# One core, a hybrid mLSTM / gMLP / memory-attention layer with experts: the second half of the memory keys in two units of 512 rows by 512 columns, and a different order of gate weights, gate rows and outputs in one DMA queue

## The reference

```
mk_p, mv_p = memory_kv(mem_prompt, mem_norm_g, w_mem_k, w_mem_v)   # rmsnorm(mem) @ w_k, @ w_v: (256 x 1024) @ (1024 x 1024) each
z = rmsnorm(x) @ w_in                     # 1024 x 10248: q,k,v,o, gate columns i,f, u, gv, memory queries, branch gates
ig = i_raw + i_b; lf = log_sigmoid(f_raw + f_b)      # 4 heads, cumulative sum and running maximum over time
...                                       # mLSTM scan, gMLP, attention of the memory queries over mk, mv
x = x + mixed @ w_out
x = x + hier_moe(rmsnorm(x), ...)         # 4 groups x 8 experts, top 2
```

## Time and profile before

| | before |
|---|---|
| median of 3 executions | 840.59 us (840.16 to 841.1) |
| profiled execution, its own time | 841.19 us |
| profiled execution, span from the first to the last instruction | 839.4 us |
| PE, DVE, ACT busy | 98%, 70%, 56% of the span |
| mean granted TensorE clock | 0.998 |

### The profile page before, as it was taken

The page is one execution under the profiler, slowest core; times in us unless marked ns, Lnnn a source line. Parts: engine busy times, 40 slices in busy tenths (PEclk is TensorE's granted clock), DMA queues, the critical chain, the costliest instruction groups (busy, mean ns, idle before and its releaser), DMA issues. The chain is left out here.

```text
span 839.4 us, 12162 instructions
## 1 busy us (share of the span) xinstructions
PE 823.4 (98%) x4744; PEld 732.3 (87%) x4744; DVE 586.7 (70%) x820; ACT 469.1 (56%) x622; POOL 62.8 (7%) x113
## 2 busy tenths in 40 slices
PE   7999999999999999999999999999999999999995
PEld 7979989988989998899999999878888888888884
DVE  5665487773445456695565456778989889889894
ACT  5645577754333324554333336656877768767773
POOL 1000100010000000000000000020004102210410
PEclk9999999999999999999999999999999999999999
DMA  8659855327534536345436467589999999999970
GB/s 269 208 142 291 221 142 132 118 81 220 165 126 126 176 115 199 126 151 163 152 110 216 151 201 256 209 264 409 389 357 351 358 397 381 352 373 366 382 279 18
DMA packets 111841, 191.83 MB, mean 229 GB/s; under 512 B 18692, under 2 KB 76960, under 8 KB 111648
## 3 DMA queue, kind: packets, MB, share of 16 engines
q1 hardware_dynamic: 109824, 185.91, 65.0%
q0 software_dynamic: 1152, 3.41, 1.1%
q10 hardware_dynamic: 800, 1.66, 0.6%
HBM read 181.70 MB, written 10.03 MB: 228 GB/s over the span
## 5 line engine op out<-in xcount | busy, mean ns | idle before, releaser
L1643 DVE TENSOR_TENSOR w_r<-arena,w_r 128x2048 fp32r<-128x2048 f32 x96 | 217.0, 2286 | 27.6 <-ACT w_r L1239 27.6
L1634 DVE TENSOR_TENSOR unit_r<-arena,unit_r 128x2048 fp32r<-128x2048 f32 x63 | 144.3, 2291 | 131.2 <-ACT unit_r L1228 131.1
L793 PE MATMUL pj<-xn_r,unit_r 128*128 128x320 f32 x1536 | 233.2, 311 | 0.8 <-issue 0.8
L793 PEld LDWEIGHTS pj<-xn_r,unit_r 128*128 128x128 f32 x1536 | 225.6, 188 | 4.7 <-issue 3.7
L1130 PE MATMUL pj<-w_r,xg 128*128 128x512 f32 x768 | 191.0, 398 | 0.5 <-DVE xg L1627 0.4
L1239 ACT ACTIVATE w_r<-arena 128x2048 fp32r<-128x2048 f32 x96 | 180.3, 1909 | 2.7 <-DMA arena<-in_w_exp_down 2.0
L1130 PEld LDWEIGHTS pj<-w_r,xg 128*128 128x128 f32 x768 | 141.8, 188 | 31.5 <-DVE xg L1627 0.8
L1228 ACT ACTIVATE unit_r<-arena 128x2048 fp32r<-128x2048 f32 x63 | 120.9, 1919 | 44.4 <-PE pj L793 23.6
L1159 PE MATMUL pj<-w_r,hidT 128*128 128x512 f32 x384 | 93.3, 392 | 0.6 <-ACT hidT L1490 0.6
L1159 PEld LDWEIGHTS pj<-w_r,hidT 128*128 128x128 f32 x384 | 71.8, 188 | 17.0 <-issue 0.8
L793 PE MATMUL pj<-br_r,unit_r 128*128 128x320 f32 x384 | 59.6, 311 | 0.0
(11 more groups left out here) (344 smaller groups left out, 793.3 us busy)
## 6 DMA issues: line engine op xcount, KB each, us to landing
arena<-in_w_in SPq DMA_DIRECT2D x40, 1024.0 KB, 5.5
arena<-in_w_exp_gate SPq DMA_DIRECT2D x64, 512.0 KB, 4.9
arena<-in_w_exp_up SPq DMA_DIRECT2D x64, 512.0 KB, 6.7
arena<-in_w_exp_down SPq DMA_DIRECT2D x64, 512.0 KB, 5.6
arena<-in_w_mem_v SPq DMA_DIRECT2D x4, 1024.0 KB, 5.3
arena<-in_w_br_mem SPq DMA_DIRECT2D x4, 1024.0 KB, 5.1
arena<-in_w_br_mlstm SPq DMA_DIRECT2D x4, 1024.0 KB, 5.1
arena<-in_w_br_gmlp SPq DMA_DIRECT2D x4, 1024.0 KB, 4.9
```

The costliest lines, as they stand in the source:

```text
L793: last = mm(bank_of(s)[0:out_rows, 0:out_cols], l, r, start=k == 0, stop=k == len(pairs) - 1)
L1634: v.tensor_tensor(unit_part(n, 1), raw_columns(n), unit_part(n, 0), ALU.subtract).then_inc(u_lo, 1)
L1643: v.tensor_tensor(w_r[u % NS][:, 1, :], raw_w[u % NS], w_r[u % NS][:, 0, :], ALU.subtract).then_inc(m_lo, 1)
```

## The change

The units 2 and 3 (columns 512 to 1023 of `w_mem_k`) become a wide pair `memk2`, as the memory values already are: unit 2 is rows 0 to 511, unit 3 rows 512 to 1023, each by 512 columns. The number of units and of MB stays. In SP's queue `load_gate_weights` moves from ahead of unit 3 to behind unit 4; the write of the gate rows stays behind unit 10 but the read that spreads them moves behind unit 11; the memory keys are stored behind unit 11, the two maxima behind unit 12, the memory values behind unit 14; the wait ahead of the prompt keys is for the two key stores alone.

```diff
@@ -97,11 +97,12 @@
                 step(kind, u, kh, i, ring="pj", eng=engs[i], unit=n, last=i == tiles - 1, held=kh == 0, of=(kind, u, 0, i) if kh else None)
                 after(u, kh, i)
 
-    for u in range(4):
+    for u in range(2):
         n = unit("w_mem_k", u * 256)
         for i in range(2):
             step("memk", u, i, ring="pj", eng="A", unit=n, last=i == 1)
             early.pop(0)()
+    wide("memk2", "w_mem_k", 0, 1, 2, "AA", lambda u, kh, i: early.pop(0)())
     for u in range(2):
         wide("memv", "w_mem_v", 0, u, 2, "AA", lambda u, kh, i: early.pop(0)())
     step("paramsync", ring=None, eng=None)
@@ -630,22 +632,27 @@
                 sp.dma_start(wrb[:, 0:G], I["b_router_group"][0, :].partition_broadcast(128)).then_inc(s_par3, 16)
                 sp.dma_start(wrb[:, G:G + E], I["b_router_expert"][0, :].partition_broadcast(128)).then_inc(s_par3, 16)
 
-            def spread_gate_rows():
+            def write_gate_rows():
 
                 sp.wait_ge(s_g4, 1)
                 sp.dma_start(spread_rows, rb[0:H, :]).then_inc(s_rbw, 16)
+
+            def spread_gate_rows():
+
                 sp.wait_ge(s_rbw, 16)
                 sp.dma_start(rbb[:, :, :].rearrange("p h t -> p (h t)"), spread_rows.rearrange("h t -> (h t)").partition_broadcast(128)).then_inc(s_rbb, 16)
 
-            def store_memory():
+            def store_maxima():
 
                 sp.wait_ge(s_g3, 1)
                 sp.dma_start(O["mlstm_m_prompt"][0, 0, :].rearrange("(h a) -> h a", a=1), rows[0:H, R_MM, TP - 1:TP]).then_inc(s_mout, 16)
                 sp.dma_start(O["mlstm_m_sample"][0, 0, :].rearrange("(h a) -> h a", a=1), rows[0:H, R_MM, T - 1:T]).then_inc(s_mout, 16)
+
+            def store_memory(name, src):
+
                 sp.wait_ge(*done("memv", 1, 1, 1))
-                for name, src in (("mem_k_prompt", memk), ("mem_v_prompt", memv)):
-                    for i in range(2):
-                        sp.dma_start(O[name][0, 0, i * 128:(i + 1) * 128].rearrange("p h d -> p (h d)"), src[:, i, :]).then_inc(s_memout, 16)
+                for i in range(2):
+                    sp.dma_start(O[name][0, 0, i * 128:(i + 1) * 128].rearrange("p h d -> p (h d)"), src[:, i, :]).then_inc(s_memout, 16)
 
             def store_conv():
 
@@ -700,7 +707,6 @@
                     for i, (t0, rows_) in enumerate(TILES):
                         src = I["x_prompt"][0, t0:t0 + rows_, :] if i < 2 else I["x_sample"][0, :, :]
                         sp.dma_start(x_tm[0:rows_, i, :], src).then_inc(s_x, 16)
-                    load_gate_weights()
                 if n == 0:
                     continue
                 if n >= 3:
@@ -709,19 +715,26 @@
                 r0 = part[0] * 512 if part else 0
                 src = I[name][0, r0:r0 + UW // w * 128, col:col + w].rearrange("(k p) n -> p k n", p=128)
                 sp.dma_start(raw_unit[unit_slot(n)].rearrange("p (k n) -> p k n", n=w), src).then_inc(unit_full[unit_slot(n)], 16)
-                if n == 6:
+                if n == 4:
+                    load_gate_weights()
+                elif n == 6:
                     sp.dma_start(ws[:, :, :], I["gmlp_w_s"][0].rearrange("g t s -> t g s")).then_inc(s_ws, 16)
                 elif n in (8, 9):
                     load_cached_keys(n - 8)
                     load_cache_v(n - 8)
                 elif n == 10:
+                    write_gate_rows()
+                elif n == 11:
                     spread_gate_rows()
-                elif n == 11:
-                    store_memory()
+                    store_memory("mem_k_prompt", memk)
+                elif n == 12:
+                    store_maxima()
                 elif n == 13:
-                    sp.wait_ge(s_memout, 64)
+                    sp.wait_ge(s_memout, 32)
                     load_prompt_keys(0)
                     load_prompt_keys(1)
+                elif n == 14:
+                    store_memory("mem_v_prompt", memv)
                 elif n in (16, 18):
                     sp.wait_ge(s_kmT, n - 14)
                     load_cached_keys(n // 2 - 6)
@@ -890,7 +903,7 @@
                             pe.wait_ge(u_lo, 1)
                         for m, (p, q) in enumerate(PARTS):
                             last = mm(b[:, 0:256], mn_r[:, p, k, a[1] * 128:a[1] * 128 + 128], w[:, q, k, :], start=k + m == 0, stop=k == KC - 1 and m == 2)
-                elif kind == "memv":
+                elif kind in ("memk2", "memv"):
                     u, kh, i = a
                     last = project_half(s, 128, kh, 3, lambda k, m: (mn_r[:, PARTS[m][0], 4 * kh + k, i * 128:i * 128 + 128], w[:, PARTS[m][1], k, :]))
                 elif kind in ("v", "gv"):
@@ -1314,9 +1327,9 @@
                     if a == (0, 0):
                         act.wait_ge(s_rsm, 1)
                     af(memk[:, a[1], a[0] * 256:a[0] * 256 + 256], b[:, 0:256], ACT.Copy, scale=rs[:, 3 + a[1]:4 + a[1]]).then_inc(free, 1)
-                elif kind == "memv" and mine:
+                elif kind in ("memk2", "memv") and mine:
                     u, _, i = a
-                    af(memv[:, i, u * 512:u * 512 + 512], b[:, 0:512], ACT.Copy, scale=rs[:, 3 + i:4 + i]).then_inc(free, 1)
+                    af((memk if kind == "memk2" else memv)[:, i, u * 512:u * 512 + 512], b[:, 0:512], ACT.Copy, scale=rs[:, 3 + i:4 + i]).then_inc(free, 1)
                 elif kind == "mq":
                     af(mqT[:, a[0], :], b[:, 0:T], ACT.Copy, scale=QSCALE).then_inc(free, 1)
                 elif kind == "sc":
```

## The result

| | before | changed |
|---|---|---|
| median | 840.85 us (840.05 to 842.34, 6 runs) | 845.19 us (844.07 to 845.69, 6 runs) |
| profiled execution, its own time | 841.19 us | 845.69 us |
| span | 839.4 us | 843.9 us |
| mean granted TensorE clock | 0.998 | 0.994 |

The ratio is 1.0049, with a 95% interval of 1.0036 to 1.0062: the change makes the kernel about 4.3 us slower. My 842.3 and my range up to 844.2 were too low.

A forecast was written before the change was run, and what follows sets the result against it. TensorE (PE), busy 98%, was taken to bound the kernel; -1.67 us in front and +3.43 us from a longer gap ahead of unit 10 gave +1.76 us, so 842.3 us, range 839.1 to 844.2.

The forecast's parts named there:

- What bounds the kernel: Whole kernel: TensorE is busy 98%, so only PE's waits or shorter matmuls can win; two waits, 1.0 and 0.8 us.
- the chain from the gate rows: Ahead of unit 10: from the spread rows' landing through DVE and ACT to PE's start, 6.13 us.
- Part 1 and 2: Units 2 and 3: wider matmuls save about 0.5 us, the vanished wait ahead of unit 3 about 1.15; 1.67 in all.
- Part 3: Ahead of unit 10: the spreading read queues behind unit 11's megabyte, so PE starts unit 10 1.76 us later.
- Part 4: Stores in SP's queue: spreading them out and waiting for two key stores instead of four changes nothing.
- The sum: Up to unit 10 -1.67 + 3.43 = +1.76 us; behind it the kernel is the same and PE-bound; 842.3 us.
- rival B: PE's clock falls in the gap ahead of unit 10: up to 3.6 us more, 845.9 us; chance 0.10.
- Rival A: Gate rows: unit 11 does not hold the spread; it lands at 74.93, kernel 839.2 us; chance 0.13.
- C: Front: its gain does not come while the gate rows are still late, +3.43 us, 844.0 us; chance 0.06.

The follow-up runs named there:

- e2: The kernel before with one move alone, the read that spreads the gate rows put behind unit 11: 845.8 us, ratio 1.0058.
- e12: The kernel before with one move alone, the write of the gate rows ahead of unit 10's load, the spreading read right behind that load: 839.57 us.
- e1: The changed kernel with the read that spreads the gate rows back behind unit 10, directly behind their write: 839.59 us, ratio 0.9989.
- e11: The changed kernel with the spreading read issued by ACT into its own DMA queue, unit 11 still in SP's queue: 845.19 us, ratio 1.0052.
- e10: The changed kernel with 14 extra products of 320 columns at the start of PE's gap ahead of unit 10, result overwritten: 843.71 us.

## Why the prediction was wrong, point by point

**What bounds the kernel.** Right: PE-bound but for few gaps, and the gap put down to "issue" is a DVE split held by the chain from the gate rows. The chain took 84.30 - 78.23 = 6.07 us, I had 6.13.

**Part 1 and 2, the front.** In the profile the wait went and PE came 2.03 us sooner to unit 8, I had 1.67. But each profile is one execution, and the wait it won back is there in some executions only (0.3 at most in e2, 0.79 in e12, 1.04 before). Over many executions the wide units and the gate weights alone are worth nothing measurable. The error was hidden in the sum, since what one wins in front of this gap is partly given back in it.

**Part 3, the gate rows.** Right in place, and in the sum: consumer at 78.23 (I had 78.05), unit 10 at 84.30 (84.18). That the sum fits so well is in part luck. The read was issued at 70.18, 0.6 us sooner than my 70.78, and unit 11 landed at 75.1, not 75.85; but the rows landed 3.1 us behind it, which was my upper bound, where I took 2.2. The order in the queue was read rightly. What I did not see is that the order does not matter much to the read: from a queue of its own it is hardly sooner.

**Part 4.** Right: e1, which has the spread stores, is no slower, and behind unit 10 the changed kernel has no wait of PE above 0.6 us, as before.

**The sum, the step that failed.** "behind it the kernel is the same and PE-bound": it was not, for 5 us. The clock fell in the gap; I had this as rival B with a chance of 0.10, because my gap of 4.25 us was shorter than the 5 us at the end of the trace. The gap was 4.73 us, and the clock fell about 3.3 us after PE's last product, at 82.9. Every execution of the changed kernel has it by its mean clock (0.992 to 0.995, where the kernel before has 0.996 to 0.998 in 64 of the 66 executions timed beside the experiments); the mean is a blunt sign, since e2, 5 us slower, has 0.994 to 0.996. The time from PE's last matmul to the fall was no constant: 2.6 us in the profile of e2, 2.5 in e11, 1.9 in e10, 5.2 at the end of the trace of before. I took the one fall in the trace for a threshold, where it was only one case that fell after so long. The price I gave B, up to 3.6 us, was too high: the low clock lasted 5.4 us of work, not the 7.2 us of 24 matmuls at half rate, and cost 2.42 us; unit 10's 1.88 us plus that is 4.3 us over the kernel before; rival B as I wrote it would have been 845.9. The Trainium skill (TensorE: Matmul & The Clock Gate, "HAM oscillation — how this bites in real kernels") had warned of just this, a DMA wait after which work restarts cold; by this the trace agrees (granted clock 0.50 from the restart at 84.30 to 89.7), and I should have given it more weight than one tail end. With B as the forecast, 842.35 + 2.4 = 844.8, and the measured median is 845.19.

Rival A did not come (78.23, not 74.9), C neither.

## What to carry to other kernels

A gap of some microseconds on a busy PE is priced twice: as the wait, and by the matmuls behind it at half the clock; ask for both as soon as a change makes a gap longer than those that the traces show at full clock (here 1.3 us; with 2.93 us about half of the executions fell). Before moving a small or late-wanted transfer behind a large one, look who waits for it, and through whom: here 770 KB behind 1 MB held DVE, ACT and PE in turn, and another queue did not help. And a write whose answer is waited for belongs ahead of the big load, which made the best kernel of this study: 838.5 to 838.7 us, 1.7 to 1.8 under the kernel before.

## What the runs showed of the hardware

The granted clock fell with an idle stretch of PE of 4.73 us in every execution (mean clock 0.992 to 0.995), after 2.93 us in about half (three of six by their mean clock), and in one profile after 1.88 us that followed 12 small products; the profiles show no fall at gaps of 1.30 us and less. It fell 1.9 to 3.3 us after the last dense matmul in four profiles (e10, e11, e2, changed). Once down it stayed there for more than 5 us of dense work in the changed kernel (84.3 to 89.7), during which PE made 5 or 6 matmuls in 1 us where it makes 9.

A transfer of 770 KB issued 0.4 to 0.5 us behind one of 1 MB was used 8.05 us after its issue from the same DMA queue and 7.4 us from another (there with 1 MB of stores beside it), where it took 4.15 us with nothing ahead of it. In the same queue the megabyte landed in 5.3 us and the 770 KB 3.1 us behind it; from two queues they landed within 0.3 us of each other, in 8.1 and 7.3 us. A write of a few KB to DRAM was answered in 2.2 to 2.4 us ahead of the load of unit 10 and in 4.8 to 5.1 us behind it.
